# A bidirectional scan layer on one core: the gated scan's context state is made in the delta-rule scan's block

## The reference

```python
def step(S, xs):
    q_c, k_c, v_c, g_c = xs
    ...
    g_last = g_c[..., -1:, :]
    S = S * jnp.exp(g_last)[..., 0, :, None] + jnp.einsum(
        "bhcd,bhce->bhde", k_c * jnp.exp(g_last - g_c), v_c)
...
o_cf, s_cf = scan_fn(*ctx_f, s0)
o_cb, s_cb = scan_fn(*[_flip(t) for t in ctx_b], s0)
o_lf, _ = scan_fn(*lat_f, s_cf)
o_lb, _ = scan_fn(*[_flip(t) for t in lat_b], s_cb)
```

## Time and profile before

| | us |
|---|---|
| median of 3 runs | 1876.94 |
| lowest, highest | 1870.19, 1878.01 |
| the profiled execution | 1878.31 |
| its span | 1876.7 |
| TensorE busy in it | 1700.9 (91%) |
| VectorE busy | 1195.2 (64%) |
| ScalarE busy | 540.8 (29%) |
| GpSimd busy | 432.4 (23%) |

### The profile page before, as it was taken

One profiled execution on the slowest core, in us unless ns is written; L12 is line 12 of the kernel. 1 busy time (PEld: TensorE's weight loads), 2 busy tenths in 40 slices (PEclk: granted clock), 3 DMA queues, 4 the chain that ended last, 5 costly groups with the idle time before them and its releaser, 6 DMA issues. The chain is left out here.

```text
span 1876.7 us, 21827 instructions
## 1 busy us (share of the span) xinstructions
PE 1700.9 (91%) x8297; PEld 1256.3 (67%) x8297; DVE 1195.2 (64%) x1741; ACT 540.8 (29%) x873; POOL 432.4 (23%) x433
## 2 busy tenths in 40 slices
PE   8999996899949968888859967999999999999997
PEld 8754452697649955545534436888888888788786
DVE  1358776366765646676743437899899899743634
ACT  2332331661014322222232223222222222232332
POOL 3000000321013324454501113333333333300000
PEclk9999997899959988999979988999999999999999
DMA  9193324266459840000041121111111111423242
GB/s 330 44 370 124 120 101 146 70 176 157 100 163 273 230 146 22 23 12 23 0 157 52 60 76 36 56 46 46 51 51 45 47 55 34 183 98 101 90 136 89
DMA packets 201543, 194.18 MB, mean 103 GB/s; under 512 B 40677, under 2 KB 155695, under 8 KB 200044
## 3 DMA queue, kind: packets, MB, share of 16 engines
q1 hardware_dynamic: 193196, 183.21, 31.2%
q10 hardware_dynamic: 6816, 5.24, 0.9%
q0 software_dynamic: 1440, 4.46, 0.6%
HBM read 150.77 MB, written 42.11 MB: 103 GB/s over the span
## 5 line engine op out<-in xcount | busy, mean ns | idle before, releaser
L2167 PE MATMUL PS<-h2hi,whi 128*128 128x512 f32 x704 | 276.3, 393 | 17.6 <-DVE h2lo L2308 17.6
L2168 PE MATMUL PS<-h2lo,whi 128*128 128x512 f32 x704 | 275.7, 392 | 0.0
L2169 PE MATMUL PS<-h2hi,wlo 128*128 128x512 f32 x704 | 275.3, 391 | 0.0
L2321 DVE SCALAR_TENSOR_TENSOR acc<-PS,fcol,acc 128x945 f32<-128x945 f32 (+2 forms) x176 | 215.2, 1222 | 33.3 <-ACT acc L2229 27.9
L2321 DVE SCALAR_TENSOR_TENSOR act<-PS,fcol,act 128x945 f32<-128x945 f32 (+2 forms) x176 | 215.2, 1223 | 24.2 <-ACT act L2229 18.8
L371 PE MATMUL PS<-hT,wq 128*128 128x512 f32 (+1 forms) x480 | 180.5, 535 | 0.0
L2167 PEld LDWEIGHTS PS<-h2hi,whi 128*128 128x128 f32 x704 | 133.1, 189 | 47.1 <-issue 13.2
L2283 POOL TENSOR_TENSOR wlo<-wu,whi 128x1024 fp32r<-128x1024 f32 x44 | 107.7, 2450 | 238.2 <-ACT whi L2222 237.9
L2169 PEld LDWEIGHTS PS<-h2hi,wlo 128*128 128x128 f32 x704 | 133.2, 189 | 28.0
L2168 PEld LDWEIGHTS PS<-h2lo,whi 128*128 128x128 f32 x704 | 133.2, 189 | 27.4
L371 PEld LDWEIGHTS PS<-hT,wq 128*128 128x128 f32 x480 | 91.2, 190 | 88.6 <-issue 85.5
(11 more groups left out here) (266 smaller groups left out, 2760.2 us busy)
## 6 DMA issues: line engine op xcount, KB each, us to landing
wm<-in_w_mod_dram SPq DMA_DIRECT2D x24, 1024.0 KB, 7.9
wu<-in_w_up_dram SPq DMA_DIRECT2D x44, 512.0 KB, 3.8
wr<-in_w_down_dram SPq DMA_DIRECT2D x44, 512.0 KB, 3.4
wq<-in_w_in_dram SPq DMA_DIRECT2D x12, 512.0 KB, 7.7
gdn_x_image<-ztile SPq DMA_DIRECT2D x5, 1032.0 KB, 14.1
gdn_xt_image<-ztile SPq DMA_DIRECT2D x5, 1032.0 KB, 24.2
GR<-gdn_gc_rows SPq DMA_DIRECT2D x20, 256.0 KB, 4.7
gdn_w_image<-Wm SPq DMA_DIRECT2D x20, 256.0 KB, 4.1
```

The costliest lines, as they stand in the source:

```text
L2167: pe.matmul(PS[:, b + half, :], whi[k][u][:, kk, :], h2hi[kk][:, cols], start=(kk == 0), stop=False)
L2168: pe.matmul(PS[:, b + half, :], whi[k][u][:, kk, :], h2lo[:, kk, cols], start=False, stop=False)
L2169: mm = pe.matmul(PS[:, b + half, :], wlo[k][u][:, kk, :], h2hi[kk][:, cols], start=False, stop=(kk == KT - 1))
L2321: tp = v.scalar_tensor_tensor(out=t_[:, r0:r1, c0:c1], in0=up[:, r0 + dr:r1 + dr, c0 + dc:c1 + dc], scalar=tap_col(j, k, f), in1=t_[:, r0: ...
```

## The change

The gated scan's context state is made in the prologue of the delta-rule scan's block, for both context tiles and directions at once. GpSimd makes `last - g` for the four, ScalarE the exponentials, GpSimd the products with k (cEk, in buffers that belong to A); TensorE transposes them (`ctx_turn`, behind `turn` of step 0), ScalarE copies them to cKt (behind decayed(0)), TensorE multiplies with v in one go (`ctx_update`, behind y32 of step 0), and VectorE puts both tiles together in cS (behind scaled2 of step 0). ks(0) waits for VectorE's twelve instructions, since it writes the same PSUM banks. The gated scan has no context steps any more; VectorE copies cS into Sbd. h is loaded in eight tiles hg[k] of 512 KB: k = 0 to 4 at the end of SyncE's queue in the delta-rule scan, into buffers of X, XT, W and A that are free by then, and 5 to 7 at the start of the gated scan, where TensorE waits for these at k = 5 of the first gate tile. SiLUs 0 to 2 go into the last latent step, behind its last exponential; 3 to 7 stay behind the step.

```diff
+        cEk = [[place(f"cEk{i}{d}", [P, 2, P], 43 + 2 * i + d) for d in range(2)] for i in range(NC)]
+        cKt = [place(f"cKt{i}", [P, 2, 2, P], 47 + 2 * i) for i in range(NC)]
+        cS = place("cS", [P, 2, 2, P], 205)
+        cg = place("cg", [P, 2, 2], 207.25)
+        hg = [place(f"hg{k}", [P, LAT], (19, 23, 27, 35, 43, 15, 31, 39)[k]) for k in range(KT)]
+        s_ca, s_ce, s_ck, s_ct = sem("ctx_k_args"), sem("ctx_k_factors"), sem("ctx_k_decayed"), sem("ctx_k_turned")
+        s_cc, s_cu, s_cs2 = sem("ctx_k_copied"), sem("ctx_u"), sem("ctx_state")
+        s_hp = sem("h_prefetched")
...
                 if t >= NC + 2:
                     sp.wait_ge(s_o[d], t - NC - 1)
+                else:
+                    sp.wait_ge(s_cu, 1)
                 sp.dma_start(A[u][d][:, :], a_dram[c, d]).then_inc(l_a[u][d], 16)
...
-    for t in range(NT - 2, NT):
-        spill(t)
+    def h_again(k):
+        sp.dma_start(hg[k][:, :], hT_dram[:, k, :]).then_inc(s_hp, 16)
+    for d in range(2):
+        sp.wait_ge(s_vn[d], NT - 2)
+    h_again(0)
+    for d in range(2):
+        sp.wait_ge(s_y2[d], NT - 1)
+    h_again(2)
+    h_again(3)
+    for d in range(2):
+        sp.wait_ge(s_vn[d], NT - 1)
+    h_again(1)
+    spill(NT - 2)
+    for d in range(2):
+        sp.wait_ge(s_o[d], NL - 1)
+    h_again(4)
+    spill(NT - 1)
     sp.wait_ge(s_ogs, 16 * NL)
+    sp.wait_ge(s_hp, 16 * 5)
...
+    def ctx_turn():
+        for i in range(NC):
+            pe.wait_ge(s_ck, 2 * i + 2)
+            for d in range(2):
+                for p in range(2):
+                    tr = pe.transpose(PS[:, 1 + 4 * i, (2 * d + p) * P:(2 * d + p + 1) * P], cEk[i][d][:, p, :], ident[:, :])
+            tr.then_inc(s_ct, 1)
+
+    def ctx_update():
+        pe.wait_ge(s_cc, 2)
+        for i in range(NC):
+            for d in range(2):
+                c = NL + (i if d == 0 else NC - 1 - i)
+                for p in range(2):
+                    mm = pe.matmul(PS[:, 4 * d + i, 2 * p * P:2 * (p + 1) * P], cKt[i][:, d, p, :], gvtok[:, c, 2 * p * P:2 * (p + 1) * P],
+                                   start=True, stop=True)
+        mm.then_inc(s_cu, 1)
     each(turn, 0)
+    ctx_turn()
     each(y32, 0)
+    ctx_update()
     each(p32, 0)
     each(y64, 0)
     each(p64, 0)
+    pe.wait_ge(s_cs2, 12)
...
+    for i in range(NC):
+        for d in range(2):
+            a.wait_ge(s_ca, 2 * i + d + 1)
+            a.activation(cEk[i][d][:, :, :], cEk[i][d][:, :, :], ACT.Exp, scale=1.0 / 16).then_inc(s_ce, 1)
+    for d in range(2):
+        last = (NT - 1) * P + P - 1 if d == 0 else NL * P
+        a.activation(cg[:, d, :], gP[:, d, :, last], ACT.Exp, scale=1.0 / 16).then_inc(s_ce, 1)
     each(exps, 0)
     each(decayed, 0)
+    for i in range(NC):
+        a.wait_ge(s_ct, i + 1)
+        a.activation(cKt[i][:, :, :, :].rearrange("p d a n -> p (d a n)"), PS[:, 1 + 4 * i, :], ACT.Copy).then_inc(s_cc, 1)
     each(whole, 0)
...
     z.then_inc(s_yz, 1)
+    for i in range(NC):
+        for d in range(2):
+            at_ = (NL + (i if d == 0 else NC - 1 - i)) * P
+            last = at_ + (P - 1 if d == 0 else 0)
+            g.tensor_tensor(cEk[i][d][:, :, :], gP[:, d, :, last:last + 1].to_broadcast([P, 2, P]), gP[:, d, :, at_:at_ + P],
+                            ALU.subtract).then_inc(s_ca, 1)
+    for i in range(NC):
+        for d in range(2):
+            at_ = (NL + (i if d == 0 else NC - 1 - i)) * P
+            g.wait_ge(s_ce, 2 * i + d + 1)
+            g.tensor_tensor(cEk[i][d][:, :, :], gk[:, :, at_:at_ + P], cEk[i][d][:, :, :], ALU.mult).then_inc(s_ck, 1)
...
     each(scaled2, 0)
+    v.wait_ge(s_cu, 1)
+    v.wait_ge(s_ce, 2 * NC + 2)
+    for d in range(2):
+        for p in range(2):
+            for hf in range(2):
+                r, n = slice(64 * hf, 64 * hf + 64), (2 * p + hf) * P
+                v.tensor_scalar(cS[r, d, p, :], PS[r, 4 * d, n:n + P], cg[r, d, p:p + 1], None, ALU.mult).then_inc(s_cs2, 1)
+    v.wait_ge(s_cs2, 8)
+    for d in range(2):
+        for hf in range(2):
+            r = slice(64 * hf, 64 * hf + 64)
+            v.tensor_tensor(cS[r, d, :, :], PS[r, 4 * d + 1, :].rearrange("p (a b n) -> p a b n", a=2, b=2)[:, :, hf, :], cS[r, d, :, :],
+                            ALU.add).then_inc(s_cs2, 1)
...
 def unrolled(body):
-    for i in range(NC):
-        body(i, i, False)
     for i in range(NL):
-        body(i, i + NC, True)
+        body(i, i, True)
...
     gate_weights(0)
-    sp.dma_start(hT[:, :, 0:512], hT_dram[:, :, 0:512]).then_inc(s_hr, 16)
-    sp.wait_ge(s_hr, 16)
-    sp.dma_start(hT[:, :, 512:LAT], hT_dram[:, :, 512:LAT]).then_inc(s_hr, 16)
+    for k in range(5, KT):
+        sp.dma_start(hg[k][:, :], hT_dram[:, k, :]).then_inc(s_hr, 16)
...
-            if n == 0:
-                pe.wait_ge(s_hr, 16 * half + 16)
             if n or half:
                 pe.wait_ge(s_c4, 2 * n + half)
         for k in range(k0, k1):
-            mm = pe.matmul(PS[:, 3, :], ws4[n % 2][:, k, :], hT[:, k, half * 512:(half + 1) * 512],
+            if n == 0 and half == 0 and k == 5:
+                pe.wait_ge(s_hr, 48)
+            mm = pe.matmul(PS[:, 3, :], ws4[n % 2][:, k, :], hg[k][:, half * 512:(half + 1) * 512],
...
+                if l == 6 and i == NL - 1:
+                    silus(0, 3)
...
+    def silus(n0, n1):
+        a.wait_ge(s_c4, 2 * n1)
+        for n in range(n0, n1):
+            a.activation(sz[:, n, :], sz[:, n, :], ACT.Silu).then_inc(s_sz, 1)
     unrolled(body)
-    a.wait_ge(s_c4, 4 * H)
-    for n in range(2 * H):
-        a.activation(sz[:, n, :], sz[:, n, :], ACT.Silu).then_inc(s_sz, 1)
+    silus(3, 2 * H)
...
-        if not lat:
-            k_args(i, t, lat)
-            decayed(i, t, lat)
-            return
...
     for u in range(2):
-        v.memset(Qbd[u][:, :, :, :], 0.0)
+        v.memset(Qbd[u][:, :, :, :], 0.0).then_inc(s_sz0, 1)
     for d in range(2):
-        v.memset(Sbd[d][:, :, :, :], 0.0).then_inc(s_s2[d], 1)
-    v.wait_ge(s_s2[1], 1)
-    v.wait_ge(s_s2[0], 1)
+        v.memset(Sbd[d][:, :, :, :], 0.0).then_inc(s_sz0, 1)
+    v.wait_ge(s_sz0, 4)
+    for d in range(2):
+        for hf in range(2):
+            r = slice(64 * hf, 64 * hf + 64)
+            cp = v.tensor_copy(Sbd[d][r, :, hf, :], cS[r, d, :, :])
+        cp.then_inc(s_s2[d], 1)
...
-    for i in range(NC):
-        body(i, i, False, False)
     with v.Fori(0, NL // 2) as i:
-        body(i, i + NC, True, True)
+        body(i, i, True, True)
     with v.Fori(NL // 2, NL) as i:
-        body(i, i + NC, True, False)
+        body(i, i, True, False)
```

More of the change, by code:

```diff
@@ L1540, in program @@
         s_o2, s_u2, s_s2 = two("gla_o"), two("gla_u"), two("gla_state")
-        s_og2 = sem("o_of_backward_added")
+        s_og2, s_sz0 = sem("o_of_backward_added"), sem("block_diagonals_zeroed")
         ND = LEVELS + 1
         def unrolled(body):
-            for i in range(NC):
-                body(i, i, False)
             for i in range(NL):
-                body(i, i + NC, True)
+                body(i, i, True)
         def cols(d, i, lat):
@@ L1702, in k_args @@
                         last = at_ + (P - 1 if d == 0 else 0)
-                        if lat or i:
+                        if t:
                             g.wait_ge(s_kde[d], t)
-                            g.sem_inc(s_tkg, 1)
                         g.tensor_tensor(Ek[d][:, :, :], gP[:, d, :, at(last, 1)].to_broadcast([P, 2, P]),
@@ L1746, in body @@
                             decayed(i, t, lat)
-                scan(g, body)
+                unrolled(body)
             @block.vector
```

## The result

| | before | after |
|---|---|---|
| median, us | 1877.47 (4 runs, 1870.19 to 1878.92) | 1896.20 (4 runs, 1891.11 to 1900.17) |
| profiled execution, its span | 1878.31, 1876.7 | 1899.29, 1897.7 |

The changed kernel is slower: ratio 1.0100, 95% interval 1.0084 to 1.0116. Forecast were 1874.3 us and "within 0.5%", with a range up to 1882. It is 18.7 us slower by the medians, 21.0 by the spans. On the page the chain of waits says as little as before: its first line, which answers to the earlier trace rows, moved by one point, and what it names is still the feed-forward part.

The account below looks back on a forecast made before the run. It took blocks run one after another, each bounded by its last event, with TensorE in the chain nearly throughout. Terms -15.6 + 15.4 - 2.4 = -2.6 us from 1876.9 gave 1874.3 us, range 1866 to 1882.

Parts of the forecast that it names:

- Step 1: Gated scan's start: without the two context steps the first level product comes earlier, a gain of 15.6 us (15.0 to 16.0).
- Step 2: Reloads of h, in the delta-rule scan's queue and at the gated scan's start: cost nothing, range 0 to 1 us.
- Step 3: Delta-rule scan's prologue, where the context state is now made: ks(0) comes later, a net loss of 15.4 us (14.5 to 20.3).
- the 1.9 us that the clock was to give back: Delta-rule scan, ks(0) to vnew(0): TensorE expected at full clock after a 10 us burst, -1.9 us.
- rival B's first part: Clock falls to half ahead of ks(0), with at most two other falls: sum +0.8, 1877.7 us; chance 0.27.
- rival B: Half clock comes back in TensorE's gaps, ahead of ks(0) and between latent steps; costs some 1.5 us in vnew(0); chance 0.35.
- Step 4: Gated scan's end: three of eight SiLUs move into the last latent step, the block ends 2.4 us earlier, VectorE late next.
- at the old pitch: Gated scan: the latent steps were expected to keep their time from one step to the next.
- Rival B's far end: Gated scan: clock falls in all seven gaps instead of one, 8.4 us more, sum +9.2, 1886 us; chance 0.08.
- Rival A: Delta-rule scan's prologue is hidden, key copies not waiting behind the decay rows: 7.1 us earlier, sum -9.7, 1867.2 us; chance 0.1.

Follow-up runs that it names:

- Experiments 1: The kernel before, with GpSimd's latent steps of the gated scan written out instead of a hardware loop: 1898.5 us, ratio 1.0097.
- Experiment 2: The changed kernel with GpSimd's hardware loop again over latent steps 1 to 7 of the gated scan, step 0 written out: 1877.4 us, ratio 1.0007.
- 10: The kernel of the first of 8 and 9, with GpSimd's latent steps written out again: 1882.1 us, ratio 1.0030 to the kernel before.
- experiment 3: The changed kernel with three idle 512-column products on TensorE behind each latent step but the last: 1873.5 us, ratio 0.9978.
- 5: The changed kernel, steps still written out, with three extra semaphore increments by GpSimd ahead of its Kt product of every level: 1885.8 us, ratio 1.0047.
- experiment 7: The changed kernel with ScalarE's two key copies ahead of the decay rows' exponentials in the delta-rule scan's prologue: 1884.4 us, ratio 1.0034.
- the first of 8 and 9: The changed kernel with GpSimd's loop again, key copies first and the context state added up in one PSUM accumulation: 1859.7 us, ratio 0.9925.
- experiment 6: The kernel before, GpSimd's loop kept, with VectorE's Qbd products of the fifth and sixth level made in four halves: 1890.2 us, ratio 1.0074.

## Why the prediction was wrong

**Step 1** (forecast -15.6) held: -15.0. Four copies took 1.21 us (forecast 1.2). The two Qbd products took 1.29 us where the row they were read from has 0.85: GpSimd's Kt now runs beside them.

**Step 2** (nothing) held. No level or gate product waits for h, and a spill, issued at 695.72, is still the last transfer of the delta-rule block, as in the earlier trace rows.

**Step 3** (forecast +15.4) was +18.5. The order of events was right; ks(0) came 31.1 us behind the block's start where 30.0 was forecast. The key copies were 0.8 later than forecast, VectorE's twelve took 4.8 us where 4.5 was the term. The larger part is the 1.9 us that the clock was to give back: ks(0) to vnew(0) took 4.50 us, as before (4.39), at half clock. The outcome is that of rival B's first part, but its cause is not: the clock did not fall in the 3.64 us ahead of ks(0), it fell 2.2 us before them, while TensorE worked at the solves. Windows (columns as above), from full clock to half:

```profile
557.75:561.10 3.35, 2.57 (x65) 1.96 (x64) 1.95 (x7) 0.00 (x0) 0.00 (x0) 1.00 0.03 5
561.15:563.30 2.15, 2.15 (x22) 1.97 (x20) 1.54 (x6) 0.38 (x1) 0.00 (x0) 0.50 0.62 182
```

So the premise that failed is "a burst of 10 us ahead of ks(0), so I expect full clock there". The 1.5 us that rival B feared for vnew(0) did not come (2.05 us).

**Step 4** (forecast -2.4) held, with the engine that is late next.

These four come to +1.1 us where the forecast had -2.6. The latent steps add 22.7 us, and -2.9 in untouched blocks makes up the 21.0 of the spans. Those 22.7 us are the step that failed: the prediction went through the change part by part and left out one part, GpSimd's loop, and so had no term for the latent steps and took them "at the old pitch". Experiments 1, 2 and 10 put the whole of it on that edit. What it does has two steps: GpSimd is 0.06 us earlier at one place, VectorE 0.57 us later (0.57 x 8 = 4.6 us), and TensorE's clock then falls at each of the seven gaps (2.8 us each, less the 1.4 that the one fall cost before). The first is shown by experiments 1 and 5, the share of the clock by experiment 3; why the first brings the second is open.

**Rival B's far end** had the mechanism, not the cause or the size. It counted every gap at 1.4 us, from the one fall in the trace, but after each fall here the half clock lasted 6.8 us instead of 3.4. And it asked only where the new start puts the gaps, with a chance of .08. Experiment 2 has the changed kernel's start (its first product 6.03 us behind its block's start, against 6.04) and keeps the clock in six of seven. The three kernels with the loop and the old steps had their first product at 705.4, 701.5 and 689.3 us and one fall each, the three written out at 708.9, 706.4 and 693.7 and seven each: so the start alone did not bring it. The Trainium skill's rule that was set beside it there (TensorE: Matmul & The Clock Gate, "HAM oscillation") came true in the changed kernel, seven gaps of seven, and not in the kernel before, one of seven. That one was read as an argument against it; in this kernel the same gap fell every time once the step had changed.

**Rival A** would have been right about the order: experiment 7 gives 9.4 us for it, where 7.1 was worked out.

**Two slips in the sums** changed nothing: steps 1 and 3 together span -1.5 to +5.3 us by their own bounds, not -1.3 to +5.5, and by its own terms step 3 would cost 0.6 us less, not 0.7, with the figures of the Trainium skill that it gives (VectorE: DVE Perf Modes, "The TRN2 errata").

**Open.** What decides whether a given gap falls. Counting a gap whose half clock begins in it or within 1.5 us of its end, one of seven fell with a warm step of 30.7 us (before, experiment 2 and the first of 8 and 9), six at 30.8 (5), six at 31.3 (6 and 7), seven in 1, in 10 and in the changed kernel. So the length of the warm step is not a measure of it: 0.1 us more came with six falls. When the steps begin matters as well: at a warm step of 31.3 us three starts gave seven falls and a fourth, that of 7, gave six, and at 30.7 the one fall was at the first gap in one trace and at the last in two. A step that fell is longer itself, too, which moves the next gap. What rule joins these is not shown. Why the half clock lasts 3.4 us in one case and 6.8 in another is open too. Nor was it tried why the written-out code starts Kt 0.06 us sooner.

## What to carry to other kernels

Go through the diff by engine and ask of every line what it does to each step of a loop, above all of the lines that look like a rewriting: 0.06 us on an engine that is mostly idle cost 20 us here. Where TensorE has a gap of the same length in every step, and the granted clock fell in one, price the case that it falls in all, and try idle products in the gap before anything else. Order work in a prologue by what it waits for: the same copies cost 9.4 us more behind a DMA wait than ahead of it.

## What the runs showed of the hardware

A gap of TensorE ahead of a step, 3.4 to 3.5 us long by its rows, may or may not be followed by half clock; with three idle products in it (wait 0.9 us left) none fell in 21 gaps of three kernels. Half clock after a fall lasted 3.4 us or 6.8 us in these steps, each us of it costing 0.4 us (0.5 in experiment 6). The clock also fell with no such gap ahead: in the changed kernel's prologue it fell at 561.1 us, while TensorE worked at solves of 64x64 blocks; the longest wait shortly ahead of it was 0.64 us. GpSimd is busy 23% of the span, yet a start of its Kt product 0.06 us sooner decides whether VectorE's two products take 1.38 or 1.95 us.
